# A mixer's attention and closing: the scan's half of the first output projection made in the attention for eleven of twelve groups, modulation blocks in pairs

## What is computed

```python
def _even_mixer(h_ctx, h_lat, ...):
    gq, gk, gv, gog, gz, aq, ak, av = _split(h @ w_in, EVEN_SIZES)
    ...
    a = _gated_readout(scan_forward + scan_backward, gog, gla_out_norm)   # 512 features: rms norm per head, times the gate
    b = _softmax_attend(qa, k, v)                                         # 8 heads of 64: 512 features
    return concatenate([a, b])

m = split(silu(c) @ mod_w[l] + mod_b[l], 6)       # modulation vectors: shifts, scales and gates
x = x + m[2] * _rms(o @ w_out, norm_post_mix[l])  # w_out: 1024 x 1024
h = _modulate(_rms(x, norm_pre_ffn[l]), m[3], m[4])
```

## Time and profile before

| | us |
|---|---|
| median of three runs | 4062.31 |
| the three runs | 4047.28, 4062.31, 4062.79 |
| profiled execution | 4048.89 |
| its span, first to last instruction | 4047.2 |
| mean granted TensorE clock of the span | 0.985 |

### The profile page before, as it was taken

The page is one execution under the profiler, slowest core; times in us unless marked ns, Lnnn a source line. Parts: engine busy times, 40 slices in busy tenths (PEclk is TensorE's granted clock), DMA queues, the critical chain, the costliest instruction groups (busy, mean ns, idle before and its releaser), DMA issues. The chain is left out here.

```text
span 4047.2 us, 50229 instructions
## 1 busy us (share of the span) xinstructions
PE 3863.9 (95%) x20101; PEld 2345.7 (58%) x20101; DVE 1751.0 (43%) x3239; ACT 854.2 (21%) x1675; POOL 695.4 (17%) x512
## 2 busy tenths in 40 slices
PE   7998899999999999999999999999999999999988
PEld 4565445555448666578844777777646545433333
DVE  2345355524764555456475566553244313111111
ACT  3214330000121333210013333331134201000000
POOL 0002212222420111033342333220003100000000
PEclk9999999999999999999999999999999999999999
DMA  5106324312542110155353110002400417999999
GB/s 182 42 1 215 109 85 144 126 62 90 176 133 66 32 47 27 63 199 177 115 188 91 28 33 25 27 30 99 139 1 1 167 45 293 417 422 422 422 421 370
DMA packets 323933, 579.89 MB, mean 143 GB/s; under 512 B 59148, under 2 KB 189420, under 8 KB 323576
## 3 DMA queue, kind: packets, MB, share of 16 engines
q1 hardware_dynamic: 323704, 576.69, 39.3%
HBM read 566.03 MB, written 10.60 MB: 142 GB/s over the span
## 5 line engine op out<-in xcount | busy, mean ns | idle before, releaser
L3598 PE MATMUL dn_ps<-room,dn_w 128*128 128x512 f32 (+1 forms) x616 | 228.8, 517 | 0.5 <-DVE dn_v_tok L4171 0.3
L1053 PE MATMUL ffn_up_ps<-room 128*128 128x384 f32 (+1 forms) x704 | 203.9, 432 | 0.0
L1053 PE MATMUL ffn_up_ps<-ffn_up_t,room 128*128 128x384 f32 (+1 forms) x704 | 198.4, 435 | 0.0
L5228 PE MATMUL experts_ps<-experts_ring,experts_xs 128*64 128x512 f32 (+1 forms) x768 | 163.2, 576 | 24.3 <-DMA experts_ring<-in_w_up 24.3
L2875 PE MATMUL hgrn_ps<-room,hgrn_w 128*128 128x512 f32 x372 | 170.4, 593 | 2.5 <-DMA hgrn_w<-in_odd_w_in 1.6
L5228 PE MATMUL experts_ps<-experts_ring,room 128*64 128x512 f32 (+1 forms) x768 | 160.5, 569 | 8.1 <-DMA experts_ring<-in_w_up 8.1
L5319 DVE TENSOR_TENSOR x_sb<-x_sb,experts_ps 128x512 f32<-128x512 f32 x56 | 38.5, 688 | 297.8 <-PE experts_ps L5160 297.8
L1053 PEld LDWEIGHTS ffn_up_ps<-room 128*128 128x128 f32 x704 | 133.8, 190 | 55.7
L1053 PEld LDWEIGHTS ffn_up_ps<-ffn_up_t,room 128*128 128x128 f32 x704 | 132.4, 190 | 56.8 <-issue 3.1
L3598 PEld LDWEIGHTS dn_ps<-room,dn_w 128*128 128x128 f32 x616 | 112.5, 191 | 75.6 <-issue 66.4
L1372 PE MATMUL ffn_down_ps<-ffn_down_w_sums,ffn_w 128*128 128x512 f32 x330 | 152.8, 599 | 0.0
(11 more groups left out here) (734 smaller groups left out, 7342.0 us busy)
## 6 DMA issues: line engine op xcount, KB each, us to landing
experts_ring<-in_w_gate SPq DMA_DIRECT2D x128, 704.0 KB, 15.1
experts_ring<-in_w_up SPq DMA_DIRECT2D x128, 704.0 KB, 17.3
experts_ring<-in_w_down SPq DMA_DIRECT2D x160, 512.0 KB, 14.1
ffn_w<-in_ffn_w_down SPq DMA_DIRECT2D x37, 1024.0 KB, 4.9
att_wm<-in_mod_w SPq DMA_DIRECT2D x12, 2048.0 KB, 9.2
ffn_w<-in_ffn_w_up SPq DMA_DIRECT2D x22, 1024.0 KB, 8.1
ffn_front<-in_ffn_w_down SPq DMA_DIRECT2D x18, 1024.0 KB, 4.8
ffn_hid<-in_mod_w SPq DMA_DIRECT2D x32, 512.0 KB, 3.6
```

Source lines behind the costliest of these rows:

```text
L1053: mm = nc.tensor.matmul(result(n, p), lhs[:, k, :], rhs[:, k, :], start=k == 0, stop=k == half - 1)
L3598: mm = nc.tensor.matmul(out, ahead.tile[:, k, :] if k < by_ahead else wt[:, h % 2, piece, k, :], hT[:, k, tok], start=k == 0, stop=k == KD ...
L5228: mm = nc.tensor.matmul(ps[out_rows, 3 * n + c, 0:b - a], xs_now[:, j, at:at + SLOTS], ring[:, w_at + a:w_at + b], start=j == 0, stop=j == ...
```

## The change

In the attention every slot's work is now named in a table (`SLOT_WORK`). `MODS` is two modulation blocks in one slot, a pair (t, b) is the half of tile t for column block b, `None` an empty slot. So the halves are eleven: both column blocks of tiles 0 to 4 and the first of tile 5. The half of column block 1 is written to columns 512 to 1023 of `scan`, where the gate stood. The ten blocks that are left after the opening go in five pairs: in the first slot of the first, third and last pair of heads, the second slot of the second pair, and the fourth of the last. A pair of blocks shares one bank and one add of VectorE, and is done as one for the semaphores, so both next loads are issued behind it. In a fifth slot of the last pair stands the half of tile 5. `half_w` holds both column blocks, 2 MB in two DMAs, at the old place in SyncE's order; the room `early` grows from 2304 to 4096 floats per partition.

In the closing `begun` becomes a pair, (4, 11): for groups 0 to 10 `k` 0 to 3 are left out, in group 11 all 8 matmuls stay. The wait for the weights' upper rows moves to group 11. For groups 6 to 10 VectorE adds out of PSUM into `y` before ScalarE squares (from `y`), and the add stands in front of L841 in VectorE's order.

```diff
@@ closing @@
-..., begun=0):
+..., begun=(0, 0)):
+    begun, begun_units = begun
...
                         pe.wait_ge(S["o_taken_d"], i + 1)
-                    for k in range(0 if j else begun + n_ahead, kt):
+                    for k in range((begun if u < begun_units else 0) + (0 if j else n_ahead), kt):
...
-                            if j and i == 0 and k == k0:
+                            if j and k == k0 and u == max(j * n_tiles, begun_units if part == 0 else 0):
                                 pe.wait_ge(S["w_in"][2 * (j % ring) + part], arrived[j][part])
...
-                        mm = nc.tensor.matmul(..., start=k == 0, stop=k == kt - 1)
+                        mm = nc.tensor.matmul(..., start=k == (begun if j and u < begun_units else 0), stop=k == kt - 1)
@@ closing, scalar @@
-                        if begun and j == 0:
-                            act.wait_ge(S["whole"], i + 1)
+                        if u < begun_units:
+                            act.wait_ge(S["whole"], u + 1)
...
-                        nc.scalar.activation(junk[:, 0:wd], y[:, t, c:c + wd] if begun and j == 0 else ps[:, u % BANKS, 0:wd], ACT.Square, ...)
+                        nc.scalar.activation(junk[:, 0:wd], y[:, t, c:c + wd] if u < begun_units else ps[:, u % BANKS, 0:wd], ACT.Square, ...)
@@ closing, vector @@
             def gated(u, j, t, c, wd):
-                if begun and j == 0:
-                    dve.wait_ge(S["mm_done"], u + 1)
-                    nc.vector.tensor_tensor(y[:, t, c:c + wd], ps[:, u % BANKS, 0:wd], y[:, t, c:c + wd], ALU.add).then_inc(S["whole"], 1)
+                if u < begun_units:
                     dve.wait_ge(S["squared"], u + 1)
...
                     u = j * n_tiles + i
+                    if u < begun_units:
+                        dve.wait_ge(S["mm_done"], u + 1)
+                        nc.vector.tensor_tensor(y[:, t, c:c + wd], ps[:, u % BANKS, 0:wd], y[:, t, c:c + wd], ALU.add).then_inc(S["whole"], 1)
                     if last and gain is not None:
@@ even_attention @@
+    MODS = "mods"
+    SLOT_WORK = ((MODS, None, None, (0, 0), (0, 1)), ((1, 0), MODS, None, (1, 1), (2, 0)), (MODS, (2, 1), None, (3, 0), (3, 1)), (MODS, (4, 0), (4, 1), MODS, (5, 0)))
...
-        return (0, 1, 3, 4) if j + 1 < PAIRS else (0, 1, 2, 3)
+        return [at for at, what in enumerate(SLOT_WORK[j]) if what]
...
-        early = sb("early", 2 * N + TILES * P)
+        early = sb("early", 2 * SH * SW)
...
-        half_w = early[:, 0:SH * SW].rearrange("p (k n) -> p k n", k=SH)
+        half_w = early[:, :].rearrange("p (b k n) -> p b k n", b=2, k=SH)
...
-        work = [("mod", m) for m in range(OPENING)]
+        work, next_mod = [("mod", (m, m + 1)) for m in range(OPENING)], OPENING
         for j in range(PAIRS):
             for at in mod_at(j):
-                scanned = 2 * j + at - 3
-                work.append(("half", scanned) if at >= 3 and j < TILES // 2 else ("mod", sum(what == "mod" for what, _ in work)))
+                if SLOT_WORK[j][at] == MODS:
+                    work.append(("mod", (next_mod, next_mod + 2)))
+                    next_mod += 2
+                else:
+                    work.append(("half", SLOT_WORK[j][at]))
...
-        at_work = [n for n, (what, _) in enumerate(work) if what == "mod"]
+        at_work = [n for n, (what, of) in enumerate(work) if what == "mod" for _ in range(*of)]
@@ even_attention, sync @@
-                    sp.dma_start(half_w, scan_w).then_inc(S["half_in"], 16)
+                    for b in range(2):
+                        sp.dma_start(half_w[:, b, :, :], scan_w[:, :, b * SW:(b + 1) * SW]).then_inc(S["half_in"], 16)
@@ even_attention, tensor: modulate @@
                 if what == "half":
-                    pe.wait_ge(S["half_in"], 16)
+                    t, b = of
+                    pe.wait_ge(S["half_in"], 32)
                     for k in range(SH):
-                        mm = nc.tensor.matmul(ps[:, bank, :], hT[:, k, m * P:(m + 1) * P], half_w[:, k, :], ...)
+                        mm = nc.tensor.matmul(ps[:, bank, :], hT[:, k, t * P:(t + 1) * P], half_w[:, b, k, :], ...)
...
-                mod = chunks[m][0]
-                pe.wait_ge(S["mod_in"][m % 2], 16 * (m // 2 + 1))
-                for k in range(KD):
-                    for g in range(MOD_GROUPS):
-                        mm = nc.tensor.matmul(ps[MOD_ROWS[g], bank, 0:MOD_PART], ...)
+                for i, m in enumerate(range(*of)):
+                    mod = chunks[m][0]
+                    pe.wait_ge(S["mod_in"][m % 2], 16 * (m // 2 + 1))
+                    for k in range(KD):
+                        for g in range(MOD_GROUPS):
+                            mm = nc.tensor.matmul(ps[MOD_ROWS[g], bank, i * MOD_PART:(i + 1) * MOD_PART], ...)
                 mm.then_inc(S["mod_mm"], 1)
@@ even_attention, vector: modulated @@
-                    nc.vector.tensor_copy(scan[:, m, 0:SW], ps[:, bank, :]).then_inc(S["mod_out"], 1)
+                    t, b = of
+                    nc.vector.tensor_copy(scan[:, t, b * SW:(b + 1) * SW], ps[:, bank, :]).then_inc(S["mod_out"], 1)
...
-                nc.vector.tensor_tensor(ot[:, m, :], ps[:, bank, 0:MOD_PART], ot[:, m, :], ALU.add).then_inc(S["mod_out"], 1)
+                flat = ot[:, m0:m1, :].rearrange("p m c -> p (m c)")
+                nc.vector.tensor_tensor(flat, ps[:, bank, 0:(m1 - m0) * MOD_PART], flat, ALU.add).then_inc(S["mod_out"], 1)
@@ first_block @@
-               ..., tokens, out0_jobs[0][0][0][0][1][:, :, 0:512], gla, out0.load)
+               ..., tokens, out0_jobs[0][0][0][0][1][:, :, 0:D], gla, out0.load)
...
-                ..., ahead=out0, then=front.load, begun=KD // 2)
+                ..., ahead=out0, then=front.load, begun=(GLA_HEADS, TILES + 5))
```

More of the change, by code:

```diff
@@ L529, in load, with closing @@
             sp.dma_start(dst, src, allow_slow_non_contiguous=True).then_inc(self.sem, 16)
-def closing(nc, tag, xT, kt, jobs, x, y, hT, ident, gate, norm, tile0=0, width=512, ring=3, readout=None, ahead=None, then=None, router=None, begun=0):
+def closing(nc, tag, xT, kt, jobs, x, y, hT, ident, gate, norm, tile0=0, width=512, ring=3, readout=None, ahead=None, then=None, router=None, begun=(0, 0)):
     mod_g, gate_at, gain = gate
     gain_n, mod_n, shift_at, scale_at = norm
+    begun, begun_units = begun
     jobs = list(jobs)
@@ L677, in _ @@
                                 pe.wait_ge(S["first_in"][n], 16 * (len(v[k0 >= kt // 2]) if type(v) is tuple else 1))
-                        mm = nc.tensor.matmul(ps[:, u % BANKS, 0:wd], xT[:, k, t * P:(t + 1) * P], wt[:, j % ring, k, 0:wd], start=k == 0, stop=k == kt - 1)
+                        mm = nc.tensor.matmul(ps[:, u % BANKS, 0:wd], xT[:, k, t * P:(t + 1) * P], wt[:, j % ring, k, 0:wd], start=k == (begun if j and u < begun_units else 0), stop=k == kt - 1)
                     mm.then_inc(S["mm_done"], 1)
@@ L751, in _ @@
                             act.wait_ge(S["squared"], u)
[L752 removed]
+                        nc.scalar.activation(junk[:, 0:wd], y[:, t, c:c + wd] if u < begun_units else ps[:, u % BANKS, 0:wd], ACT.Square, accum_out=parts[:, t, j:j + 1]).then_inc(S["squared"], 1)
                     if j == blocks - 1:
@@ L2306, in modulate @@
             def modulate(n, bank=7):
-                what, m = work[n]
+                what, of = work[n]
                 if n >= len(OPENING_BANKS):
@@ L3326, in first_block @@
         closing(nc, "out0", hT, KD, out0_jobs, x, mix, hT, ident,
-                (mods[0], 2, I["norm_post_mix"][0]), (I["norm_pre_ffn"][0], mods[0], 3, 4), ahead=out0, then=front.load, begun=KD // 2)
+                (mods[0], 2, I["norm_post_mix"][0]), (I["norm_pre_ffn"][0], mods[0], 3, 4), ahead=out0, then=front.load, begun=(GLA_HEADS, TILES + 5))
         later0 = Modulation(sc, 0, I["mod_w"][1], I["mod_b"][1], mods[1], 4, 12)
```

18 lines of the change are left out of this document (9 added, 9 removed).

## The result

| | us |
|---|---|
| median after, 20 runs | 4065.43 (4059.06 to 4074.28) |
| median before, 20 runs beside them | 4055.39 (4045.64 to 4062.79) |
| ratio | 1.0028, 95% interval 1.0022 to 1.0034 |
| profiled execution after, its span | 4074.28, 4072.5 |

The change costs 11.4 us (8.9 to 13.8). The forecast was +11.0 and 4066. The profiled execution of after is the slowest of its 20, 9 us above their median, so its stretches read a little long; a second profile of the same kernel stands with the experiments.

What follows compares the result with a forecast made beforehand. TensorE was taken to bound the attention and last block, VectorE second. Attention +18.4 us and closing -7.4 gave +11.0, added to the middle of four executions, 4055.6: 4066 us, range 4050 to 4082.

Steps and rivals of the forecast that it cites:

- the wait in the first pair: First slot: TensorE waits 4.1 us (3.8 to 4.4) for the second block's weights, behind one more MB of loads.
- First pair, +7.6: First head pair of the attention: 1.87 for the doubled slot, 4.1 wait, 1.6 lower clock, together 7.6 us more.
- The empty slot: First pair's second slot loses its block but gains nothing; transposes behind it wait 2.04 us for GpSimd instead of 0.17.
- The slow block, 1.6 us: First pair's second block after the weights wait: the clock may fall, costing 1.6 us or nothing; 1.6 taken.
- Second and third pair, +3.3 each: Attention: each pair gets one half more (+1.57) and two blocks in one slot (+1.87); +3.3 us each, 6.6 together.
- Last pair, +4.2: Last head pair: three more halves (10.4 us) and small waits, less weights waits, slow block and GpSimd's wait; 38.8 us long.
- Closing, -7.4: Last block: five groups lose 4 matmuls each, 17.1 us of TensorE; VectorE's chain lets 7.4 us through.
- TensorE is in time: Closing: TensorE's sixth group starts at 544.2 after a turn and ends at 551.1, before VectorE's sixth row at 555.6.
- A: Rival, closing: VectorE does not bound the last block, all 17.1 us are saved; +1.3 us in all, chance 0.08.
- B: Rival, first pair: the additional MB is hidden and the clock stays; +6.5 us in all, chance 0.12.
- C: Rival, last pair: next stage's weights delay both blocks by 2 us, slow block behind; +3.6, 14.6 in all, chance 0.12.
- D: Rival, closing: clock falls between groups and is low in the sixth; +9.0, in all +20.0 us, chance 0.13.

Runs made afterwards that it cites:

- filler: Changed kernel plus 10 filler matmuls of 128 x 256 between the first pair's two blocks, where TensorE waits for weights; 1.0027 (+11 us) against the kernel before.
- closing_no_adds: Kernel before's attention slots, changed closing without the additions in groups 6 to 10, part of the result left out; 0.9962 (-15 us) against the kernel before.
- closing_only: Kernel before's attention slots with single blocks and six halves, changed kernel's closing, part of the result left out; 0.9987 (-5 us) against the kernel before.
- spread: Kernel before's work with the ten modulation blocks placed singly in spread slots, half_w loading 2 MB; 0.9984 (-6 us) against the kernel before.

## Why the prediction was right, step by step

**The sum** was +11.0 and the runs say +11.4. The mechanisms held: the wait in the first pair, the waits of the last pair gone, and VectorE as the limit of the closing. That the two numbers agree so closely is in part luck. By the two profiles the five stages cost 18.7 and 14.9 us more than in the profile of before, not 11.0, and the clearest misses, the closing and the third pair, both went to the costly side. The sum of the profiles is too high, as the profile of before was one of its shorter runs and the clock fell at places where it had not; how the 11.4 us divide among the stages in a middling run is not shown.

**First pair, +7.6.** Right in kind, +8.5 in the quieter profile and +11.8 in the other; counted from the first slot on, +7.4 and +10.6. The 1.1 us before that slot are a clock that fell behind a wait of 3.2 us for VectorE. The earlier trace rows show the same wait of before with the clock at 1.00, and I took from it that such a wait may cost nothing. In twelve of the fourteen profiles of this case it did cost: what follows starts at the lower clock (0.54 in the first profile of the changed kernel). The wait was put at 4.1 and is 3.9 and 5.05 us. With the megabyte loaded later it is still 1.65 and 2.67, where I had put 1.2. The landing was worked out from bytes at the full rate; in the first profile 344 to 347.4 moved at 122 GB/s, the tail of a load with none behind it:

```profile
335.00:341.00 6.00, 5.41 (x44) 3.81 (x48) 3.78 (x6) 3.05 (x7) 2.79 (x1) 0.72 1.04 390
341.00:344.00 3.00, 1.30 (x48) 0.97 (x40) 1.06 (x4) 2.06 (x4) 2.43 (x1) 1.00 1.05 386
344.00:347.40 3.40, 0.05 (x4) 0.05 (x8) 0.00 (x0) 0.00 (x0) 0.20 (x1) 0.75 0.34 122
```

The empty slot: forecast 2.04 us of GpSimd's wait, found 0.78 + 1.18 = 1.96. The slow block, 1.6 us: seen (3.46 and 3.60 against 1.93, so 1.5 and 1.7). With the filler the block took 1.93 us and the time stayed at +11; whether the 1.6 us can be won back stays open.

**Second and third pair, +3.3 each.** Second +3.1 in both profiles. Third +4.6 in both, with the clock low once (0.96 by the window, 0.74 from 454 to 460.5); that fall was in no step. Without it the third pair is 43.8 us in three other profiles with the same slots, +2.9.

**Last pair, +4.2.** +5.3, and 38.68 us, so +4.1, in the second profile. Three halves at 3.44 us are 10.3 and not 10.4, so the terms add up to 4.1 as well. The loads were in time.

**Closing, -7.4.** -6.1 and -5.4. Step by step VectorE's part held: 1.47 us from addition to L843, 6.14 us a group, and the additions as the cause by closing_no_adds. What failed is "TensorE is in time": I let a turn wait for VectorE's row alone and left out that it also waits for the copies of the turn before. So the sixth group starts 4.04 us behind the fourth group's L843 (569.57 to 573.61) and its own L843 is 1.0 us late. In the second profile the fifth group, at a clock of 0.59, is late as well, and L843 is 1.8 us late. The last 0.4 and 0.2 us come from the first block, where VectorE starts later by that much, held by the load of its column constants.

**The Trainium skill's rule** on the clock (TensorE: Matmul & The Clock Gate, HAM oscillation): the trace agrees that the clock falls behind such a wait, to 0.50 behind the 5.05 us (347.4 to 350.8) as in the earlier trace rows; no run shows that avoiding the wait alone brings the time back.

**The rivals.** A (TensorE bounds the closing) is out by closing_only, -5 us and not -17. B (the megabyte is hidden) is out by the waits of 3.9 and 5.05 us against 1.65 and 2.67. C (the stall of the last pair stays) is out: no wait there. D (the clock low in the sixth group) did not come: it ran at full clock (7.03 us); groups four and five did run slow (5.29 us), as D had it, and had cover in the first profile, but not wholly in the second, where the fifth took 5.91 us and cost 0.8.

**The base of the forecast.** I took four times for two levels and added to their middle. The 98 later runs of the kernel before fill the space between: there are no two levels. That the middle, 4055.6, met the median of 20 runs, 4055.4, was luck.

## What to carry to other kernels

In this case work moved into another stage's slots was paid there in full unless the slot had a hole, and saved at the old place only down to the next engine's chain. Price both sides before such a move. To cure a wait for a load, space out the work that needs it; two items in one slot need two loads at once, and the slot left empty opens the hole that its work covered. When a busy engine gets less to do, write down every wait of the engine that comes next, those on buffers too.

## What the runs showed of the hardware that was not expected

The spread of a kernel's runs goes with the granted clock of the whole span. Over the 98 runs of the kernel before that stand beside the experiments, the correlation is -0.88 and the slope about 2.9 us per 0.001: 4058.2 to 4064.2 us in the five runs at 0.981, 4046.9 to 4056.0 in the 33 at 0.984 and 4044.7 to 4049.2 in the nine at 0.986. The falls stand at other places from run to run, so a stage's length in one profile can be 3 us off: the first pair of the changed kernel was 52.5 and 49.3 us. And the length of a wait did not settle whether the clock fell: after the same 3.2 us for VectorE at the start of the first pair it was at 1.00 in two profiles (before and spread) and low in twelve, and it fell after 1.95 us as well (spread, the block at 329.55: 3.58 us, clock 0.50).
